# x times g fed to the first 27 projection units in quarters, with 1/rms applied to their products

## The chip, the cores and the metric

One core of a Trainium2 chip runs the whole kernel. The time is the device time of that core in microseconds (us); less is better. Before the change it is 2242.05 us, the median of 3 runs.

## What is computed

One inference step of a decoder layer with two token mixers, in float32. There are 288 tokens (256 of a prompt, 32 of 8 sampled sequences of 4) and D_MODEL is 2048. What matters here is how it begins:

```
h    = x * rsqrt(mean(x*x) + 1e-6) * g_mix          # RMSNorm, per token
proj = h @ w_in                                     # all projections of both mixers
pb       = proj[..., N_IN_A:]                       # 3360 columns: 3 LoRA inputs, r, k, v
pb_first = h_prev @ w_in[:, N_IN_A:]                # h_prev: state_shift, already normalised
pb_prev  = concat([pb_first, pb[:, :-1]])
xm       = pb + (pb_prev - pb) * mu_b               # token shift
```

Then come the RWKV-7 state, sparse attention with an indexer, two branch projections, a gated merge, an output projection, and a SwiGLU block. h of each sequence's last token is an output too (shift).

## The kernel before

Everything is transposed: partitions are channels, tokens are columns. The weights come as units of 128 output channels, 1 MB each (128 partitions by 16 k-tiles of 128 columns), through a ring of four slots in SBUF. SyncE issues their loads, each when the unit four before it has been read. The first 27 units (3 for the LoRA inputs, 8 each for r, k and v) are those whose product is mixed with that of the previous token; they are the part that the change touches.

A unit of these is a float32 product in three passes. ScalarE copies the weight to a rounded upper half (`first_high`, L953), VectorE subtracts to get the lower half, in place in the ring (`first_low`, L1382), and TensorE does, for each k-tile, upper by upper, lower h by upper weight, and upper h by lower weight (`first_unit`, L454 to L456), 48 matmuls into one of two PSUM banks. The columns are NX = 296: the 288 tokens and 8 columns of state_shift.

Then ScalarE copies the product, shifted by one token, from PSUM to SBUF (`previous`, L974 to L976), and VectorE does the mixing with two operations that read the bank (`mix`, L1413 and L1415), the second of which frees it. Only then may TensorE fill that bank with the unit after the next. The upper halves of the weights have two buffers, so `first_high(u + 2)` waits until unit u has been read. All order is by counting semaphores and by the order of the code on each engine.

What comes ahead of unit 0: SyncE loads x (L309), the constants, the parameters (g_mix among them), the 8 state columns, the page table and the LoRA weights, and then units 0 to 3. ScalarE squares x in four pieces (L948), TensorE sums the squares over channels with a matrix of ones (`total_squares`, L466, which waits for all the small loads, since the ones are among the constants), VectorE forms the mean (L1366), ScalarE the root (L961), VectorE the reciprocal (L1368), and then VectorE forms h with one operation for each k-tile (`normed`, L1371), ScalarE its upper half (L964) and VectorE the lower (`first_h_low`, L1386), in groups of four k-tiles.

```
for u, dst in enumerate((SW, SG[:, 0, :], SG[:, 1, :])):
    first_low(u + 2, u + 3)
    mix(u, u % 2, dst)
```

After unit 7's load SyncE fetches 16 pages of indexer keys (L346), and goes on with unit 8. After unit 26, TensorE does the LoRA products (L486), ScalarE their sigmoids (L1001), and a long chain on VectorE follows (from L1444).

## Time and profile before

| | |
|---|---|
| median of 3 runs | 2242.05 us (2241.3 to 2242.24) |
| profiled execution, its time | 2239.98 us |
| profiled execution, its span | 2237.8 us |
| mean granted TensorE clock | 0.955 |
| TensorE (PE) busy | 2086.7 us, 93% |
| VectorE (DVE) busy | 1007.9 us, 45% |
| ScalarE (ACT) busy | 738.5 us, 33% |
| GpSimd (POOL) busy | 36.8 us, 2% |

The span is the stretch from the first to the last recorded instruction; the execution's time is 2.2 us longer. The engines work side by side, so their busy times don't add up. Since matmuls are pipelined, a busy TensorE is not TensorE at its peak. PEld is the load of weights into the array, SPq the issuing of transfers by SyncE.

### The profile page before, as it was taken

How to read it: one execution, taken by the hardware profiler on the slowest of the kernel's cores; microseconds unless marked ns; L12 is line 12 of the kernel's file. 1: busy time of each engine (PE TensorE's matmuls, PEld its weight loads, DVE VectorE, ACT ScalarE, POOL GpSimd, SP SyncE). 2: the span in 40 equal slices, each digit the busy share in tenths (PEclk: the TensorE clock that was granted, in tenths of full speed). 3: DMA queues.
4: the chain of work that ended last, by engine and by line, in shares of the span. 5: the costliest groups of instructions: out<-in, count | busy, mean ns of one | idle time of the engine just before them, and what ended most of it. 6: DMA issues, size and time to landing. Idle time of an engine off the chain costs nothing.

```text
span 2237.8 us, 38450 instructions
## 1 busy us (share of the span) xinstructions
PE 2086.7 (93%) x15718; PEld 1862.7 (83%) x15718; DVE 1007.9 (45%) x1161; ACT 738.5 (33%) x953; POOL 36.8 (2%) x59
## 2 busy tenths in 40 slices
PE   5999967999998989988998997999999999999996
PEld 4999745658885855558998997999999999999995
DVE  4454966717665601024454344444444444333333
ACT  3333202352323200023443233444454444233332
POOL 0000002100000000000000000000000000000000
PEclk9999987899998998888999998999999999999998
DMA  5444353324531399973445452444444444554452
GB/s 190 158 167 152 111 187 98 84 87 142 176 125 66 105 379 362 369 287 113 169 165 196 145 198 91 160 164 166 169 169 165 160 164 167 172 167 160 163 168 81
DMA packets 96821, 375.69 MB, mean 168 GB/s; under 512 B 27954, under 2 KB 38834, under 8 KB 69234
## 3 DMA queue, kind: packets, MB, share of 16 engines
q1 hardware_dynamic: 70626, 335.36, 43.0%
q10 hardware_dynamic: 21152, 19.66, 2.7%
q0 software_dynamic: 4976, 19.71, 2.5%
q8 instruction: 49, 0.80, 0.1%
q14 instruction: 18, 0.15, 0.0%
HBM read 358.14 MB, written 16.53 MB: 167 GB/s over the span
## 4 chain that ended last, share of the span: by engine, by line
PE 85%; DVE 7%; DMA 3%; ACT 2%; issue 2%; SPq 2%; ACTq 0%; POOL 0%; DVEq 0%; POOLq 0%
PE ps L420 13%; PE ps L912 13%; PE ps L913 13%; PE ps L914 12%; PE ps L871 5%; PE ps L872 4%; PE ps L873 4%; PE ps L454 2%; PE ps L455 2%; PE ps L456 2%; PE ps L812 2%; PE ps L844 1%; DMA gram<-arena 1%; PE ps L856 1%; PE ps L576 1%
## 5 line engine op out<-in xcount | busy, mean ns | idle before, releaser
L1766 DVE TENSOR_TENSOR weights_lo<-ring,weights_hi 128x2048 fp32r<-128x2048 f32 (+1 forms) x152 | 305.5, 2010 | 466.2 <-ACT weights_hi L1314 466.2
L912 PE MATMUL ps<-h_hi,weights_hi 128*128 128x288 f32 x1408 | 415.4, 295 | 15.4 <-DVE h_lo L1775 15.4
L913 PE MATMUL ps<-h_lo,weights_hi 128*128 128x288 f32 x1408 | 416.9, 296 | 0.0
L914 PE MATMUL ps<-h_hi,weights_lo 128*128 128x288 f32 x1408 | 413.3, 294 | 0.0
L420 PE MATMUL ps<-hT,ring 128*128 128x288 f32 x1472 | 381.2, 412 | 1.2 <-ACT arena L1083 1.2
L1314 ACT ACTIVATE weights_hi<-ring 128x2048 fp32r<-128x2048 f32 (+1 forms) x152 | 257.0, 1691 | 342.5 <-PE ps L914 341.0
L420 PEld LDWEIGHTS ps<-hT,ring 128*128 128x128 f32 x1472 | 273.8, 191 | 79.8 <-issue 7.0
L912 PEld LDWEIGHTS ps<-h_hi,weights_hi 128*128 128x128 f32 x1408 | 265.0, 188 | 15.8 <-DVEq L1790 15.8
L914 PEld LDWEIGHTS ps<-h_hi,weights_lo 128*128 128x128 f32 x1408 | 265.8, 189 | 0.0
L913 PEld LDWEIGHTS ps<-h_lo,weights_hi 128*128 128x128 f32 x1408 | 265.2, 188 | 0.0
L912 PE MATMUL ps<-act_hi,weights_hi 128*128 128x288 f32 x704 | 209.1, 297 | 4.9 <-DVE act_lo L1800 4.9
L913 PE MATMUL ps<-act_lo,weights_hi 128*128 128x288 f32 x704 | 208.3, 296 | 0.0
L914 PE MATMUL ps<-act_hi,weights_lo 128*128 128x288 f32 x704 | 207.5, 295 | 0.0
L1683 DVE TENSOR_TENSOR weights_lo<-ring,mix_weights_hi 128x2048 fp32r<-128x2048 f32 x48 | 110.0, 2292 | 143.3 <-ACT mix_weights_hi L1245 143.3
L454 PE MATMUL ps<-first_h_hi,first_weights_hi 128*128 128x296 f32 x432 | 131.2, 304 | 14.3 <-DVE first_h_lo L1386 10.6
L1245 ACT ACTIVATE mix_weights_hi<-ring 128x2048 fp32r<-128x2048 f32 x48 | 91.8, 1913 | 141.3 <-PE ps L873 141.3
L912 PEld LDWEIGHTS ps<-act_hi,weights_hi 128*128 128x128 f32 x704 | 132.5, 188 | 5.1 <-issue 5.1
L914 PEld LDWEIGHTS ps<-act_hi,weights_lo 128*128 128x128 f32 x704 | 133.2, 189 | 0.0
L913 PEld LDWEIGHTS ps<-act_lo,weights_hi 128*128 128x128 f32 x704 | 132.8, 189 | 0.0
L455 PE MATMUL ps<-first_h_lo,first_weights_hi 128*128 128x296 f32 x432 | 131.1, 303 | 0.0
L456 PE MATMUL ps<-first_h_hi,weights_lo 128*128 128x296 f32 x432 | 130.5, 302 | 0.0
L1382 DVE TENSOR_TENSOR weights_lo<-ring,first_weights_hi 128x2048 fp32r<-128x2048 f32 x27 | 61.9, 2292 | 106.8 <-ACT first_weights_hi L953 106.8
(333 smaller groups left out, 3041.0 us busy)
## 6 DMA issues: line engine op xcount, KB each, us to landing
ring<-in_wst SPq DMA_DIRECT2D x201, 1024.0 KB, 4.8
ring<-in_wdn SPq DMA_DIRECT2D x64, 704.0 KB, 4.0
arena<-in_kT SPq DMA_DIRECT2D x64, 512.0 KB, 5.5
arena<-in_v SPq DMA_DIRECT2D x64, 512.0 KB, 6.0
ring<-in_wst ACTq DMA_DIRECT2D x8, 1024.0 KB, 7.9
arena<-chunk_ar_bk ACTq DMA_DIRECT2D x24, 256.0 KB, 3.5
arena<-in_ki SPq DMA_DIRECT2D x64, 64.0 KB, 1.8
chunk_ar_bk<-arena POOLq DMA_DIRECT2D x2, 2048.0 KB, 14.3
```

Of the source, the lines that this page charges most:

```text
L420: ins = mm(out, ring[:, slot, k, :], rhs(k), start=(k == 0), stop=(k == KT - 1))
L454: mm(out, W_HI1[:, (u0 + s) % 2, w], H_HI1[:, k, :], start=(k == 0), stop=False)
L455: mm(out, W_HI1[:, (u0 + s) % 2, w], H_LO1[:, k, :], start=False, stop=False)
L456: ins = mm(out, W_LO[:, slot, w], H_HI1[:, k, :], start=False, stop=(k == KT - 1))
L871: mm(out, MW_HI[:, (u - U_MIX) % 2, w], hi, start=start, stop=False)
L912: mm(out, W_HI[:, (u - U_FF) % 2, w], hi, start=start, stop=False)
L913: mm(out, W_HI[:, (u - U_FF) % 2, w], lo, start=False, stop=False)
L914: return mm(out, W_LO[:, u % 4, w], hi, start=False, stop=stop)
L1245: fn(MW_HI[:, (u - U_MIX) % 2], ring[:, u % 4].rearrange("p k c -> p (k c)"), ACT.Copy).then_inc(sem("mix_w_high"), 1)
L1314: fn(W_HI[:, (u - U_FF) % 2, 0:n], ring[:, u % 4].rearrange("p k c -> p (k c)")[:, 0:n], ACT.Copy).then_inc(sem("w_high"), 1)
L1683: tt(W_LO[:, u % 4], raw, MW_HI[:, (u - U_MIX) % 2].bitcast(F32), ALU.subtract).then_inc(sem("mix_w_split"), 1)
L1766: tt(W_LO[:, u % 4, 0:m], raw, W_HI[:, at, 0:m].bitcast(F32), ALU.subtract).then_inc(sem("w_split"), 1)
```

## The change

x is loaded in four quarters of four k-tiles, each with its 8 state columns, behind the parameters and with unit 0's weight between the second and the third; the constants, the page table and the LoRA weights come behind unit 3. The units are fed not with h but with x times g: ScalarE forms the upper half of x times g (a copy with g as its scale), VectorE the lower half in one operation from x, g and the upper half. 1/rms is a factor of each token, so it may be applied to the product: `scaled` (L1442) multiplies a unit's bank by it on the way from PSUM to one of two SBUF buffers (NRM) and frees the bank, and `previous` and `mix` read NRM. For the state columns the factor is 1. The squares are made by GpSimd; TensorE sums the first half of them ahead of unit 0 and the second between units 0 and 1, with a matrix of ones that VectorE sets. h itself, which later stages need, is formed by VectorE two k-tiles a unit in units 3 to 10, and the shift output is taken at unit 11. VectorE's loops over the units are written out.

```
-        RSTD = area(33216, NT)
-        XT = area(16384, KT, NT)
+        XT = area(16640, KT, NX)
...
-        LAST = area(16384 + 4608, KT, 1 + NB)
+        LAST, ONE1 = area(23680, KT, 1 + NB), area(23840, P)
+        NRM, RSX = area(28672, 2, NX), area(29264, NX)
...
-            sp.dma_start(XT, xT[:, :, 0:NT]).then_inc(sem("x_in"), 16)
-            sp.dma_start(cst[:, :], cst_d).then_inc(sem("const_in"), 16)
-            sp.dma_start(prm[:, :], prm_d).then_inc(sem("const_in"), 16)
-            sp.dma_start(hT[:, :, NT:NX], xT[:, :, NT:NX]).then_inc(sem("const_in"), 16)
-            sp.dma_start(ptab[:, :], pt_d).then_inc(sem("const_in"), 16)
-            sp.dma_start(LORA, lora_d[0]).then_inc(sem("lora_in"), 16)
-
...
-            for u in range(4):
+            def x_group(g):
+
+                sp.dma_start(XT[:, 4 * g:4 * g + 4, :], xT[:, 4 * g:4 * g + 4, :]).then_inc(sem(f"x_in{g}"), 16)
+
+            sp.dma_start(prm[:, :], prm_d).then_inc(sem("prm_in"), 16)
+            x_group(0)
+            x_group(1)
+            unit(0, 0)
+            x_group(2)
+            x_group(3)
+            for u in range(1, 4):
                 unit(u, u)
+            sp.dma_start(cst[:, :], cst_d).then_inc(sem("const_in"), 16)
+            sp.dma_start(ptab[:, :], pt_d).then_inc(sem("const_in"), 16)
+            sp.dma_start(LORA, lora_d[0]).then_inc(sem("lora_in"), 16)
             units(4, 8, unit)
-            sp.wait_ge(sem("const_in"), 64)
-            sp.wait_ge(sem("h_done"), 1)
+            sp.wait_ge(sem("const_in"), 32)
...
-                        pe.wait_ge(sem("first_h_split"), k // 4 + 1)
+                        pe.wait_ge(sem("first_h_split"), 5 * (k // 4 + 1))
...
+            def squares_group(g):
+
+                pe.wait_ge(sem("squares"), g + 1)
+                for k in range(4 * g, 4 * g + 4):
+                    ins = mm(ps[7][:, 0:NT], ONE1, SQ[:, k, :], start=(k == 0), stop=(k == KT - 1))
+                if g == 3:
+                    ins.then_inc(sem("squares_summed"), 1)
+
             pe.sem_inc(sem("bank_free"), 2)
             pe.sem_inc(sem("chunk_done"), 1)
-            pe.wait_ge(sem("const_in"), 64)
-            total_squares(0, SQ)
-            for u in range(3):
-                first_unit(u, 0, 0)
+            pe.wait_ge(sem("dve_chain"), 1)
+            squares_group(0)
+            squares_group(1)
+            first_unit(0, 0, 0)
+            squares_group(2)
+            squares_group(3)
+            first_unit(1, 0, 0)
+            first_unit(2, 0, 0)
...
+            pe.wait_ge(sem("const_in"), 32)
+            pe.wait_ge(sem("h_done"), 1)
...
-            act.wait_ge(sem("x_in"), 16)
-            squares(XT, SQ)
+            def first_h_high(g):
+
+                act.wait_ge(sem(f"x_in{g}"), 16)
+                for k in range(4 * g, 4 * g + 4):
+                    fn(H_HI1[:, k, 0:NT], XT[:, k, 0:NT], ACT.Copy, scale=p_("g_mix", k)).then_inc(
+                        sem("first_h_high"), 1)
+                fn(H_HI1[:, 4 * g:4 * g + 4, NT:NX], XT[:, 4 * g:4 * g + 4, NT:NX], ACT.Copy).then_inc(
+                    sem("first_h_high"), 1)
+
+            act.wait_ge(sem("prm_in"), 16)
+            first_h_high(0)
+            first_h_high(1)
             first_high(0)
+            first_h_high(2)
+            first_h_high(3)
             first_high(1)
+            act.wait_ge(sem("unit_read"), 1)
+            first_high(2)
             act.wait_ge(sem("mean_sq"), 1)
-            fn(RSTD, RSTD, ACT.Sqrt).then_inc(sem("root"), 1)
-            for g in range(4):
-                act.wait_ge(sem("h_group"), g + 1)
-                fn(H_HI1[:, 4 * g:4 * g + 4, :], hT[:, 4 * g:4 * g + 4, :], ACT.Copy).then_inc(
-                    sem("first_h_high"), 1)
+            fn(RSX[:, 0:NT], RSX[:, 0:NT], ACT.Sqrt).then_inc(sem("root"), 1)
...
             def previous(u, par):
-                act.wait_ge(sem("unit_read"), u + 1)
-                act.wait_ge(sem("bank_free"), u + 1)
-                bank, pv = ps[par], PV[:, par, :]
+                act.wait_ge(sem("bank_free"), u + 3)
+                bank, pv = NRM[:, par, :], PV[:, par, :]
...
             for u in range(3):
-                act.wait_ge(sem("unit_read"), u + 1)
-                first_high(u + 2)
+                if u:
+                    act.wait_ge(sem("unit_read"), u + 1)
+                    first_high(u + 2)
+                if u == 2:
+                    act.wait_ge(sem("mixed"), 1)
                 previous(u, u % 2)
-            act.wait_ge(sem("bank_free"), 2 + 3)
+            act.wait_ge(sem("mixed"), 3)
             fn(SW[0:64, :], SW[0:64, :], ACT.Tanh).then_inc(sem("act_stage"), 1)
             ch(fn(SG, SG, ACT.Sigmoid))
             with act.Fori(0, 5) as i:
                 for s in range(4):
                     act.wait_ge(sem("unit_read"), i * 4 + (U_RKV + s + 1))
                     first_high(U_RKV + s + 2, i, 4)
+                    act.wait_ge(sem("mixed"), i * 4 + (U_RKV + s - 1))
                     previous(i * 4 + (U_RKV + s), (U_RKV + s) % 2)
...
-                rstd = RSTD if n == 0 else SG[:, 0, :]
+                rstd = SG[:, 0, :]
...
             def normed(dst, src, g, k):
-                return stt(dst[:, k, 0:NT], src[:, k, :], p_(g, k), RSTD if g == "g_mix" else SG[:, 0, :],
+                return stt(dst[:, k, 0:NT], src[:, k, 0:NT], p_(g, k), RSX[:, 0:NT] if g == "g_mix" else SG[:, 0, :],
                            ALU.mult, ALU.mult)
 
+            ch(nc.vector.memset(ONE1, 1.0))
+            ch(nc.vector.memset(RSX, 1.0))
...
             def first_h_low(g):
-                dve.wait_ge(sem("first_h_high"), g + 1)
-                tt(H_LO1[:, 4 * g:4 * g + 4, :], hT[:, 4 * g:4 * g + 4, :],
-                   H_HI1[:, 4 * g:4 * g + 4, :].bitcast(F32), ALU.subtract).then_inc(sem("first_h_split"), 1)
-
+                dve.wait_ge(sem("first_h_high"), 5 * (g + 1))
+                for k in range(4 * g, 4 * g + 4):
+                    stt(H_LO1[:, k, 0:NT], XT[:, k, 0:NT], p_("g_mix", k), H_HI1[:, k, 0:NT].bitcast(F32), ALU.mult,
+                        ALU.subtract).then_inc(sem("first_h_split"), 1)
+                old = slice(4 * g, 4 * g + 4)
+                tt(H_LO1[:, old, NT:NX], XT[:, old, NT:NX], H_HI1[:, old, NT:NX].bitcast(F32),
+                   ALU.subtract).then_inc(sem("first_h_split"), 1)
+
+            first_h_low(0)
+            first_h_low(1)
             first_low(0, 1)
-            first_low(1, 2)
-            dve.wait_ge(sem("const_in"), 64)
-            inv_rms(0)
-            for k in range(KT):
-                ins = normed(hT, XT, "g_mix", k)
-                if k % 4 == 3:
-                    ins.then_inc(sem("h_group"), 1)
-                else:
-                    ch(ins)
-                if k in (7, 11):
-                    first_h_low(k // 4 - 1)
-            dve.wait_ge(sem("h_group"), 4)
             first_h_low(2)
             first_h_low(3)
-            ch(cp(LAST[:, :, 0:1], hT[:, :, SEQ - 1:SEQ]))
-            cp(LAST[:, :, 1:], hT[:, :, SEQ:NT].rearrange("p k (b t) -> p k b t", t=NS)[:, :, :, NS - 1]).then_inc(
-                sem("h_done"), 1)
-
-
-            def mix(u, par, dst, rows=P):
+            first_low(1, 2)
+            dve.wait_ge(sem("squares_summed"), 1)
+            ts(RSX[:, 0:NT], ps[7][:, 0:NT], 1.0 / DM, EPS, ALU.mult, ALU.add).then_inc(sem("mean_sq"), 1)
+            first_low(2, 3)
+            dve.wait_ge(sem("root"), 1)
+            ch(nc.vector.reciprocal(RSX[:, 0:NT], RSX[:, 0:NT]))
+
+            def scaled(u):
+                dve.wait_ge(sem("unit_read"), u + 1)
+                tt(NRM[:, u % 2, :], ps[u % 2][:, 0:NX], RSX, ALU.mult).then_inc(sem("bank_free"), 1)
+
+            def mix(u, dst):
                 dve.wait_ge(sem("previous"), u * 3 + 3)
-                dve.wait_ge(sem("bank_free"), u + 2)
-                bank = ps[par][:, 0:NT]
-                ch(tt(DIF, PV[:, par, :], bank, ALU.subtract))
-                mu = prm[:, bass.ds(u + PRM["mu"][0], 1)]
-                stt(dst, DIF[0:rows], mu[0:rows], bank[0:rows], ALU.mult, ALU.add).then_inc(sem("bank_free"), 1)
+                if u:
+                    dve.wait_ge(sem("mixed"), u)
+                now = NRM[:, u % 2, 0:NT]
+                ch(tt(DIF, PV[:, u % 2, :], now, ALU.subtract))
+                stt(dst, DIF, p_("mu", u), now, ALU.mult, ALU.add).then_inc(sem("mixed"), 1)
 
             def flat(a):
                 return a.rearrange("p a n -> p (a n)")
 
-            for u, dst in enumerate((SW, SG[:, 0, :], SG[:, 1, :])):
-                first_low(u + 2, u + 3)
-                mix(u, u % 2, dst)
-            with dve.Fori(0, 4) as i:
-                ch.enter(i, 4)
-                for s in range(4):
-                    first_low(U_RKV + s + 2, i * 4 + (U_RKV + s + 3))
-                    mix(i * 4 + (U_RKV + s), (U_RKV + s) % 2, flat(RK[:, bass.ds(i * 4 + s, 1), :]))
-            ch.leave(4)
-            for j in range(CT):
-                u = U_RKV + 2 * CT + j
-                if u + 2 < U_IDX:
+            for u in range(U_IDX):
+                scaled(u)
+                if 3 <= u + 2 < U_IDX:
                     first_low(u + 2, u + 3)
-                mix(u, u % 2, V[:, j, :])
-            dve.wait_ge(sem("bank_free"), 2 + 27)
+                if u < 3:
+                    dst = (SW, SG[:, 0, :], SG[:, 1, :])[u]
+                elif u < U_RKV + 2 * CT:
+                    dst = RK[:, u - U_RKV, :]
+                else:
+                    dst = V[:, u - U_RKV - 2 * CT, :]
+                mix(u, dst)
+                if 3 <= u < 3 + KT // 2:
+                    for k in range(2 * (u - 3), 2 * (u - 2)):
+                        ch(normed(hT, XT, "g_mix", k))
+                if u == 3 + KT // 2:
+                    ch(cp(LAST[:, :, 0:1], hT[:, :, SEQ - 1:SEQ]))
+                    cp(LAST[:, :, 1:], hT[:, :, SEQ:NT].rearrange("p k (b t) -> p k b t", t=NS)[:, :, :, NS - 1]).then_inc(
+                        sem("h_done"), 1)
+            dve.wait_ge(sem("mixed"), U_IDX)
...
         @block.gpsimd
         def _(pool):
+            for g in range(4):
+                pool.wait_ge(sem(f"x_in{g}"), 16)
+                part = XT[:, 4 * g:4 * g + 4, 0:NT]
+                nc.gpsimd.tensor_tensor(SQ[:, 4 * g:4 * g + 4, :], part, part, ALU.mult).then_inc(sem("squares"), 1)
```

Three places of the order. First ScalarE from its start: L948 are the squares, L953 and L972 the upper halves of weights, L964 and L979 the upper halves of h or of x times g (L981 for the state columns), L961 and L994 the root. Before:

```order
L948 ACT_TABLE_LOAD
L948 ACTIVATE arena<-arena 128x1152 [waits x_in]
L948 ACTIVATE arena<-arena 128x1152 x3
L953 ACTIVATE first_weights_hi<-ring 128x2048 [waits w_in0]
L953 ACTIVATE first_weights_hi<-ring 128x2048 [waits w_in1]
L961 ACT_TABLE_LOAD
L961 ACTIVATE arena<-arena 128x288 [waits mean_sq]
L964 ACTIVATE first_h_hi<-hT 128x1184 [waits h_group] x4
```

and with the change:

```order
L979 ACT_TABLE_LOAD [waits x_in0]
L979 ACTIVATE first_h_hi<-arena,prm 128x288 [waits prm_in]
L979 ACTIVATE first_h_hi<-arena,prm 128x288 x3
L981 ACTIVATE first_h_hi<-arena 128x4x8
L979 ACTIVATE first_h_hi<-arena,prm 128x288 [waits x_in1]
L979 ACTIVATE first_h_hi<-arena,prm 128x288 x3
L981 ACTIVATE first_h_hi<-arena 128x4x8
L972 ACTIVATE first_weights_hi<-ring 128x2048 [waits w_in0]
L979 ACTIVATE first_h_hi<-arena,prm 128x288 [waits x_in2]
L979 ACTIVATE first_h_hi<-arena,prm 128x288 x3
L981 ACTIVATE first_h_hi<-arena 128x4x8
```

The squares are gone from ScalarE, the four large copies have become twenty, the first two quarters stand ahead of unit 0's weight, and the table load has the wait for the first quarter.

Second, VectorE from its first weight or lower half on. Before (L1382 lower half of a weight, L1366 and L1368 mean and reciprocal, L1371 h, L1386 its lower half):

```order
L1382 TENSOR_TENSOR weights_lo<-ring,first_weights_hi 128x2048 [waits first_high,dve_chain]
L1382 TENSOR_TENSOR weights_lo<-ring,first_weights_hi 128x2048 [waits first_high]
L1366 TENSOR_SCALAR arena<-ps 128x288 [waits squares_summed,const_in]
L1368 RECIPROCAL arena<-arena 128x288 [waits root]
L1371 SCALAR_TENSOR_TENSOR hT<-arena,prm 128x288 [waits dve_chain] x4
L1371 SCALAR_TENSOR_TENSOR hT<-arena,prm 128x288
L1371 SCALAR_TENSOR_TENSOR hT<-arena,prm 128x288 [waits dve_chain] x3
L1386 TENSOR_TENSOR first_h_lo<-hT,first_h_hi 128x1184 [waits first_h_high]
L1371 SCALAR_TENSOR_TENSOR hT<-arena,prm 128x288
```

and with the change (L1422 and L1425 lower half of x times g, L1417 of a weight):

```order
L1422 SCALAR_TENSOR_TENSOR first_h_lo<-arena,prm,first_h_hi 128x288 [waits first_h_high,dve_chain]
L1422 SCALAR_TENSOR_TENSOR first_h_lo<-arena,prm,first_h_hi 128x288 x3
L1425 TENSOR_TENSOR first_h_lo<-arena,first_h_hi 128x4x8
L1422 SCALAR_TENSOR_TENSOR first_h_lo<-arena,prm,first_h_hi 128x288 [waits first_h_high]
L1422 SCALAR_TENSOR_TENSOR first_h_lo<-arena,prm,first_h_hi 128x288 x3
L1425 TENSOR_TENSOR first_h_lo<-arena,first_h_hi 128x4x8
L1417 TENSOR_TENSOR weights_lo<-ring,first_weights_hi 128x2048 [waits first_high]
L1422 SCALAR_TENSOR_TENSOR first_h_lo<-arena,prm,first_h_hi 128x288 [waits first_h_high]
L1422 SCALAR_TENSOR_TENSOR first_h_lo<-arena,prm,first_h_hi 128x288 x3
```

Mean, reciprocal and h no longer stand ahead of the lower halves; two quarters stand ahead of unit 0's weight.

Third, VectorE in the units. Before, units 1 and 2:

```order
L1382 TENSOR_TENSOR weights_lo<-ring,first_weights_hi 128x2048 [waits first_high]
L1413 TENSOR_TENSOR arena<-arena,ps 128x288 [waits bank_free,previous]
L1415 SCALAR_TENSOR_TENSOR small<-arena,prm,ps 128x288 [waits dve_chain]
L1382 TENSOR_TENSOR weights_lo<-ring,first_weights_hi 128x2048 [waits first_high]
L1413 TENSOR_TENSOR arena<-arena,ps 128x288 [waits bank_free,previous]
L1415 SCALAR_TENSOR_TENSOR small<-arena,prm,ps 128x288 [waits dve_chain]
```

and with the change, unit 3 and the first two rows of unit 4 (L1442 is `scaled`, L1449 and L1450 the mixing, L1404 h):

```order
L1442 TENSOR_TENSOR arena<-ps,arena 128x296 [waits unit_read]
L1417 TENSOR_TENSOR weights_lo<-ring,first_weights_hi 128x2048 [waits first_high]
L1449 TENSOR_TENSOR arena<-arena 128x288 [waits mixed,previous]
L1450 SCALAR_TENSOR_TENSOR arena<-arena,prm 128x288 [waits dve_chain]
L1404 SCALAR_TENSOR_TENSOR hT<-arena,prm 128x288
L1404 SCALAR_TENSOR_TENSOR hT<-arena,prm 128x288 [waits dve_chain]
L1442 TENSOR_TENSOR arena<-ps,arena 128x296 [waits unit_read,dve_chain]
L1417 TENSOR_TENSOR weights_lo<-ring,first_weights_hi 128x2048 [waits first_high]
```

The operation that frees the bank stands ahead of the weight's lower half now, and behind it before.

## Rows read from the trace of the kernel before

**Rows 1.** The page: the chain that ended last, its shares by engine.
```profile
PE 85%; DVE 7%; DMA 3%; ACT 2%; issue 2%; SPq 2%; ACTq 0%; POOL 0%; DVEq 0%; POOLq 0%
```

**Rows 2.** Timeline, 0 to 62: start, duration, engine, line, what [idle before, releaser].
```profile
0.72 1.28 ACT L948 ACT_TABLE_LOAD   x1 [0.72 <-PEq L1935]
0.73 0.69 SPq L309 DMA_DIRECT2D arena<-in_xT  x1
...
5.91 8.21 SPq L313 DMA_DIRECT2D ptab<-in_pt  x1
10.54 4.32 ACT L948 ACTIVATE arena<-arena 128x1152 f32<-128x1152 f32 x4 [8.54 <-DMA arena<-in_xT]
...
15.17 10.53 PE L466 MATMUL ps<-arena,cst 128*128 128x288 f32 x32 [15.17 <-DMA ptab<-in_pt]
20.12 1.91 ACT L953 ACTIVATE first_weights_hi<-ring 128x2048 fp32r<-128x2048 f32 x1 [5.26 <-DMA ring<-in_wst]
22.14 2.29 DVE L1382 TENSOR_TENSOR weights_lo<-ring,first_weights_hi 128x2048 fp32r<-128x2048 f32 x1 [20.70 <-ACT first_weights_hi L953]
22.73 1.91 ACT L953 ACTIVATE first_weights_hi<-ring 128x2048 fp32r<-128x2048 f32 x1 [0.69 <-DMA ring<-in_wst]
...
27.84 1.95 DVE L1368 RECIPROCAL arena<-arena 128x288 f32<-128x288 f32 x1 [0.51 <-ACT arena L961]
29.83 4.27 DVE L1371 SCALAR_TENSOR_TENSOR hT<-arena,prm 128x288 f32<-128x288 f32 x8
...
34.02 1.38 DVE L1386 TENSOR_TENSOR first_h_lo<-hT,first_h_hi 128x1184 fp32r<-128x1184 f32 x1
...
35.55 0.58 PE L454 MATMUL ps<-first_h_hi,first_weights_hi 128*128 128x296 f32 x1 [9.85 <-DVE first_h_lo L1386]
```

**Rows 3.** Windows: stretch, length, busy (x) by engine, granted clock, DMA share, GB/s.
```profile
15.00:20.00 5.00, 4.83 (x10) 3.53 (x11) 0.00 (x0) 0.00 (x0) 0.00 (x0) 1.00 0.95 365
20.00:25.70 5.70, 5.70 (x23) 4.05 (x21) 3.32 (x2) 4.87 (x3) 0.00 (x0) 1.00 1.02 428
...
30.50:31.00 0.50, 0.00 (x0) 0.00 (x0) 0.47 (x2) 0.00 (x0) 0.00 (x0) 0.50 0.00 0
35.50:40.50 5.00, 4.95 (x19) 4.62 (x20) 4.79 (x9) 1.19 (x1) 0.00 (x0) 0.50 0.00 0
...
45.95:52.50 6.55, 6.55 (x50) 6.55 (x49) 3.17 (x3) 2.33 (x4) 0.00 (x0) 1.00 0.47 161
```

**Rows 4.** The chain in order of time at unit 8, then two windows there.
```profile
65.59 0.33 SPq L317
...
85.19 4.98 DMA ring<-in_wst
...
94.35 0.46 DVE arena L1413
94.98 0.53 DVE arena L1415
95.64 0.58 PE ps L454
...
92.30:95.00 2.70, 0.01 (x1) 0.00 (x0) 2.52 (x3) 2.57 (x7) 0.00 (x0) 1.00 0.97 388
...
96.00:98.50 2.50, 2.50 (x12) 2.50 (x12) 2.32 (x3) 0.00 (x0) 0.00 (x0) 0.50 0.48 187
```

**Rows 5.** The page's DMA issues: KB each, median us from issue to landing.
```profile
ring<-in_wst SPq DMA_DIRECT2D x201, 1024.0 KB, 4.8
...
arena<-in_ki SPq DMA_DIRECT2D x64, 64.0 KB, 1.8
```

**Rows 6.** Timeline of ScalarE and VectorE behind unit 26.
```profile
221.76 0.38 ACT L974 ACTIVATE arena<-ps 128x255 f32<-128x255 f32 x1 [6.01 <-PE ps L456]
...
222.40 7.18 ACT L1001 ACTIVATE arena<-ps,prm 128x288 f32<-128x288 f32 x16
...
236.48 14.55 DVE L1444 RECIPROCAL arena<-arena 128x2304 f32<-128x2304 f32 x1 [2.87 <-ACT arena L1005]
```

More of the change, by code:

```diff
@@ L994, in _ @@
                     first_high(u + 2)
+                act.wait_ge(sem("mixed"), u - 1)
                 previous(u, u % 2)
```

## The prediction

> **What bounds the kernel now.** The chain of waits over the whole span comes first: TensorE holds 85% of it [rows 1]. So an edit is worth what it moves the moment at which TensorE's work goes on, and nothing else. The change touches only the first 27 units (the first tenth of the span), and there I read the timeline from the start [rows 2]. The load of x is issued at 0.73 and lands at 10.54; TensorE starts at 15.17, released by the page table's load, whose issue alone held SyncE's queue from 5.91 to 14.12; the 16 products with ones take 10.53; then comes a serial stretch on VectorE: two weight splits, the reciprocal (1.95), 16 products for h at 4.27 for eight, and four lower halves of h at 1.38. TensorE's first product of unit 0 starts at 35.55.
>
> The windows show the clock [rows 3]. From 15.00 to 20.00 TensorE gets through 10 matmuls of the ones product, and in the next 5.70 through 23: half the pace, though the granted clock is printed as 1.00. TensorE fell idle at 25.7 (15.17 + 10.53); by 30.50 the granted clock is 0.50 (1.2 instead of 2.4 GHz), and it still is over the first 5.0 after TensorE's restart. After that a unit of 48 matmuls takes 6.55. Unit 0 ends at 45.95, where the row of a unit begins, so unit 2 ends at 59.05. I use that moment as the yardstick.
>
> There is one more hole, at unit 8 [rows 4]. SyncE issues unit 7's load at 65.59, then 16 pages of indexer keys, and only then, at 85.19, unit 8's. That weight's lower half is there at 94.35, and behind it VectorE does the two mixing operations of unit 6 (until 95.5) which free the PSUM bank that unit 8 wants. TensorE does next to nothing from 92.30 on, at a granted clock of 1.00 up to 95.00, restarts at 95.64, and has 0.50 from 96.00 to 98.50.
>
> **The change, part by part.** *The loads.* A 1 MB unit lands 4.8 after its issue, a 64 KB page 1.8 [rows 5]; two units in one train land 2.6 apart (20.12 and 22.73 [rows 2]). A quarter of x is 606 KB, so some 1.5 each in a train. With the parameters' load issued at 0.73 and the first quarter at about 1.2: 1.2 + 1.8 + 1.5, and 1.0 for the parameters and for the slow start of an empty queue (estimate) gives 5.5. Then 7.0 for the second quarter, 9.6 for unit 0, 11.1, 12.6, and 15.2 for unit 1. The constants, the page table and the LoRA weights come behind unit 3 and are needed much later; the page table's 8.21 of queue time would now hold back only unit 4, which can't be issued before unit 0 is read. That costs nothing.
>
> *ScalarE.* Its table load, 1.28 at 0.72 so far, now stands behind the wait for the first quarter: 5.5 to 6.8. A scaled copy of 288 elements costs 0.45 (the sigmoids, 16 in 7.18 [rows 6]) and the four samples' copies little, so 1.9 a quarter: quarters 0 and 1 by 10.6, W-high of unit 0 (1.91) by 12.5, quarters 2 and 3 by 16.3.
>
> *VectorE.* Four operations of 0.53 and a small one are 2.3 a quarter, a weight's lower half 2.29. Alone it would do quarter 0 from 8.8 to 11.1, quarter 1 by 13.4, unit 0's weight by 15.7, quarters 2 and 3 by 20.3, unit 1's weight by 22.6.
>
> *GpSimd.* Its price is in no row: in this stage it runs no elementwise operation. The lower bound is VectorE's two-operand operation, 1.38 for 1184 elements, so 1.35 for 1152; the upper one the dearest elementwise row, the reciprocal, 1.95 for 288, so 7.8. I take 2.5, near the lower end, since the operation is of the cheap row's kind. The Trainium skill (GPSIMD Engine Reference, section 3.1) gives 4.5 us for 2048 such elements, which as an estimate is 2.5 here too; no run here shows it yet.
>
> *Both together.* Squares and lower halves each read two operands from SBUF at the same time, which no stretch of this trace shows. Bounds: they don't disturb each other, or each instruction has the memory to itself and they take turns. Taking turns, the squares run 5.5 to 8.0 and 8.0 to 10.5; VectorE, ready at 8.8, gets one operation in before the third (11.0 to 13.5), one before the fourth (14.0 to 16.5), and then has quarter 0 done at 17.8, quarter 1 at 20.1, the weight at 22.4, quarter 2 at 24.7, quarter 3 at 27.0. Undisturbed it is 15.7 for the weight. No row decides between them. Since both engines would read two operands each, of the same quarters, in the same microseconds, I take turns as the likelier case, and keep both ends. The Trainium skill (SBUF — State Buffer, section on SBUF's two separate sides) says VectorE and GpSimd share one pair of ports as an exclusive lock for a whole instruction when VectorE has two SBUF inputs; no run here shows it yet.
>
> *TensorE.* The ones products for quarters 2 and 3 now stand between units 0 and 1: 8 of 16, 4.0 at full pace (23 halves of such a product in 5.70 [rows 3]). Taking turns: TensorE has been idle since about 14, so 22.5 starts at half clock. The first eight k-tiles take 5.5 (20 of 24 matmuls in 5.0 at half pace), the next two groups of 12 some 1.65 each: unit 0 ends at 31.3, the squares at 35.3, unit 1 at 41.9, unit 2 at 48.4. Against 59.05 that is 10.6 earlier. Undisturbed: start 15.8, unit 0 ends at 22.4 (quarter 3 is there at 20.3), unit 2 at 39.5, 19.5 earlier. The mean, the root, the reciprocal and the first scaling take 0.46 + 0.45 + 1.95 + 0.46 after the squares, with a 2.29 weight between them: about 6 of the 6.55 of unit 1, so unit 2's bank is free in time.
>
> *Every unit.* VectorE gains a 0.46 operation from PSUM and, in units 3 to 10, two of 0.53. It has 2.29 + 0.46 + 0.52 per 6.55 now, so 4.8 with all: covered. If it were not, the lower half of unit u+2, ready 4.4 after unit u ends, would have 2.1 to spare.
>
> *Unit 8.* The bank is freed by the scaling, ahead of the weight's split, so TensorE restarts at 94.45 in the old times: 1.2 less. The clock fell only after 95.00; if TensorE's restart comes before that and it no longer falls, the stretch at half pace, 2.5 by the window and about 3 with its edges, gives 1.5 more. I count 2.7. Ends: 1.2 and 2.7.
>
> *The end of the stage.* ScalarE's last three copies (221.76 [rows 6]) now wait for a scaling of 0.46 and its release, and the 16 sigmoids and table loads behind them lead straight to VectorE's reciprocal at 236.48. That costs 0.6; it is the one place where the change adds to the path. From there all goes on as before, earlier.
>
> **Sum.** 10.6 + 2.7 - 0.6 = 12.7. The profiled execution took 2239.98 (its span 2237.8); it would be 2227.3. The median of the three runs is 2242.05, 2.07 above, and the forecast is for a median: 2229.3.
>
> **The rivals.**
> *A, undisturbed.* GpSimd and VectorE don't hinder each other: 19.5 + 2.7 - 0.6 = 21.6, so 2220.4. For it: no engine in the trace is seen to slow another. Against it: here two engines do two-operand reads of the same tile for the first time. Between this and the forecast lies a mere slowing, some 2225.
> *B, GpSimd is dear.* All four squares stand before VectorE's lower halves when turns are taken, and each microsecond more of a square delays TensorE's first unit by four. At 5.7 a square (2.5 + 12.7 / 4) the gain is gone, at 6.8 the kernel is slower by 0.2%, at the upper bound of 7.8 unit 0's weight is split at 42.6 and the time is about 2250. For it: nothing shows GpSimd's pace. Against it: it would have to be over four times the VectorE row.
> *C, it doesn't do what it says.* The first quarter lands no earlier than the whole did, because the small parameters' load ahead of it and the queue's start take most of the 10: then only the unblocked queue and the shorter serial stretch count. Starting 5 later, at 2234.
>
> **How the numbers follow.** Taking turns as computed 0.46, A 0.30, between them 0.12, C or a price of a square up to 5 (gains of 4.5 to 9) 0.05, no change 0.03, B 0.04. Within 0.2% (4.5) is what a measurement of this kernel can't tell from no change. So faster 0.93, same 0.03, slower 0.04. The range goes from A with 2 more (an earlier landing, a warmer clock), 2218, to turns with a square of 3.5, 2233.
>
> **What would show it.** The first quarter's wait on ScalarE ends at 5 to 6. GpSimd's four squares, with their mean. VectorE's lower halves: 0.53 each if A holds, stretched or held back to about 17 if turns are taken. TensorE's first product of unit 0 at 22.5 (A: 15.8) and unit 2's end at 48.4 (A: 39.5). The hole before unit 8 is 2.1 long with the clock at 1.00 behind it. Behind unit 26, ScalarE's copies start some 0.5 later after TensorE's last product than before. Wrong would be: a hole in TensorE between units 3 and 26 that was not there, or a later stage that doesn't start earlier by the same amount.

## The result and the profile after

| | before | after |
|---|---|---|
| median | 2241.68 us (4 runs, 2240.98 to 2242.24) | 2222.45 us (4 runs, 2221.03 to 2224.28) |
| ratio | | 0.9921, 95% interval 0.9905 to 0.9938 |
| profiled execution, span | 2239.98, 2237.8 | 2222.53, 2220.6 |

The kernel became 19.2 us faster by the medians and 17.45 by the two profiled executions. A second comparison of the same two kernels, made later, gave 2220.61 (6 runs) against 2240.07 (11 runs), ratio 0.9918 (0.9901 to 0.9934). The forecast was 2229.3, range 2218 to 2233: its direction was right, and its time 6.9 too high.

The page's chain by engine answers to [rows 1]: TensorE holds the end as before, and SyncE has 1% where it had 2%.

```profile
PE 86%; DVE 7%; DMA 3%; ACT 2%; issue 1%; SPq 1%; POOL 0%; DVEq 0%; POOLq 0%; ACTq 0%
```

The timeline of after from 0 to 40 (start, duration, engine, line, what, in brackets the idle time before and the releaser), against [rows 2]:

```profile
1.18 0.90 SPq L331 DMA_DIRECT2D arena<-in_xT  x2
5.88 0.33 SPq L342 DMA_DIRECT2D ptab<-in_pt  x1
...
5.63 1.28 ACT L979 ACT_TABLE_LOAD   x1 [5.63 <-DMA arena<-in_xT]
6.93 1.81 ACT L979 ACTIVATE first_h_hi<-arena,prm 128x288 fp32r<-128x288 f32 x4
...
8.97 1.15 DVE L1422 SCALAR_TENSOR_TENSOR first_h_lo<-arena,prm,first_h_hi 128x288 fp32r<-128x288 f32 x1 [6.83 <-ACT first_h_hi L981]
8.97 2.44 DVE L1422 SCALAR_TENSOR_TENSOR first_h_lo<-arena,prm,first_h_hi 128x288 fp32r<-128x288 f32 x4 [6.83 <-ACT first_h_hi L981]
10.90 0.51 DVE L1422 SCALAR_TENSOR_TENSOR first_h_lo<-arena,prm,first_h_hi 128x288 fp32r<-128x288 f32 x1
11.43 2.36 DVE L1422 SCALAR_TENSOR_TENSOR first_h_lo<-arena,prm,first_h_hi 128x288 fp32r<-128x288 f32 x1
11.43 5.50 DVE L1422 SCALAR_TENSOR_TENSOR first_h_lo<-arena,prm,first_h_hi 128x288 fp32r<-128x288 f32 x4
16.95 2.28 DVE L1417 TENSOR_TENSOR weights_lo<-ring,first_weights_hi 128x2048 fp32r<-128x2048 f32 x1
19.16 1.79 DVE L1422 SCALAR_TENSOR_TENSOR first_h_lo<-arena,prm,first_h_hi 128x288 fp32r<-128x288 f32 x4
...
5.64 4.17 POOL L1877 TENSOR_TENSOR arena<-arena 128x1152 f32<-128x1152 f32 x2 [5.20 <-DMA arena<-in_xT]
10.97 4.79 POOL L1877 TENSOR_TENSOR arena<-arena 128x1152 f32<-128x1152 f32 x2 [1.17 <-DMA arena<-in_xT]
...
19.29 0.62 PE L459 MATMUL ps<-first_h_hi,first_weights_hi 128*128 128x296 f32 x1 [4.34 <-DVE weights_lo L1417]
28.06 4.04 PE L478 MATMUL ps<-arena 128*128 128x288 f32 x16
```

The first quarter of x lands at 5.6. Later, with GpSimd done, four lower halves of x g take 1.79 (a step of 0.43 each; a single one has a duration of 0.51). The four from 8.97 take 2.44 and the four from 11.43 take 5.50. The single rows show where: the one that starts at 8.97 ends at 10.12, which is 0.31 after GpSimd's second square is over (5.64 + 4.17 = 9.81); the one that starts at 11.43 lasts 2.36 and ends 0.31 after the third square (10.97 + 2.51 = 13.48). Between 9.81 and 10.97 GpSimd waits for the third quarter, and there VectorE gets through quarter 0: its fourth operation starts at 10.90. TensorE starts unit 0 at 19.29, not at 35.55.

The windows of after (stretch, length, busy and count by engine, granted clock, DMA share, GB/s), against [rows 3] and the clock in [rows 4]:

```profile
20.00:24.00 4.00, 4.00 (x18) 4.00 (x18) 4.00 (x10) 0.00 (x0) 0.00 (x0) 0.50 0.85 358
24.00:28.00 4.00, 4.00 (x31) 4.00 (x30) 1.07 (x1) 0.00 (x0) 0.00 (x0) 0.99 0.00 0
...
78.00:80.00 2.00, 0.00 (x0) 0.00 (x0) 1.97 (x1) 1.96 (x5) 0.00 (x0) 1.00 1.00 422
80.00:82.00 2.00, 1.62 (x12) 1.62 (x13) 1.93 (x5) 0.47 (x1) 0.00 (x0) 1.00 0.99 389
```

Unit 0 still starts at half clock (0.50, which is 1.2 GHz), until about 24. The hole at unit 8 is still there (2.4 long), but the granted clock stays 1.00 in it and behind it. The chain of after at that hole, which answers to [rows 4], and at the end of the changed stage (L503 and L486 are the LoRA products, L1034 and L1001 their sigmoids):

```profile
70.95 5.11 DMA ring<-in_wst
76.09 1.93 ACT first_weights_hi L972
78.03 2.30 DVE weights_lo L1417
...
80.38 0.40 PE ps L459
...
205.04 4.13 PE ps L503 x18
209.17 3.80 ACT arena L1034 x9
...
219.88 14.56 DVE arena L1483
```

and the chain of before at the stage's end:

```profile
221.68 4.13 PE ps L486 x18
225.81 3.76 ACT arena L1001 x9
```

The two mixing operations that stood between the lower half and TensorE are gone from the chain. The rows of ScalarE and VectorE behind unit 26, against [rows 6]:

```profile
205.66 0.41 ACT L1002 ACTIVATE arena<-arena 128x255 f32<-128x255 f32 x1 [5.91 <-DVE arena L1442]
206.19 6.78 ACT L1034 ACTIVATE arena<-ps,prm 128x288 f32<-128x288 f32 x16
219.88 14.55 DVE L1483 RECIPROCAL arena<-arena 128x2304 f32<-128x2304 f32 x1 [2.48 <-ACT arena L1038]
```

**Where the 17.45 came from.** VectorE's long reciprocal, the landmark at the end of the changed stage, starts at 219.88 instead of 236.48: 16.60 earlier. Unit 2 ends at 45.25 (there ScalarE's copy of the next weight starts) instead of 59.05, which is 13.80 of it. From TensorE's products behind unit 26 to the reciprocal it is 14.84 (from 205.04), and it was 14.80 (from 221.68): nothing gained or lost. The remaining 2.84 is the hole at unit 8. Behind the landmark the two executions take 2000.7 and 2001.3 to the span's end, and what lies outside the span is 0.25 shorter.

### The profile page after: what moved, and what is told of

It reads as the page before. It is cut to its first block, busy times and chain, and to the rows that moved or that the text cites. A ratio compares the mean times of both kernels' runs of the same rounds, so it can differ in the third digit from the quotient of the medians.

```text
span 2220.6 us, 38439 instructions
## 1 busy us (share of the span) xinstructions
PE 2084.1 (94%) x15718; PEld 1860.0 (84%) x15718; DVE 1026.8 (46%) x1206; ACT 739.0 (33%) x965; POOL 45.8 (2%) x63
## 4 chain that ended last, share of the span: by engine, by line
PE 86%; DVE 7%; DMA 3%; ACT 2%; issue 1%; SPq 1%; POOL 0%; DVEq 0%; POOLq 0%; ACTq 0%
PE ps L425 13%; PE ps L931 13%; PE ps L932 13%; PE ps L933 13%; PE ps L890 5%; PE ps L891 5%; PE ps L892 5%; PE ps L459 2%; PE ps L460 2%; PE ps L461 2%; PE ps L831 2%; PE ps L863 1%; DMA gram<-arena 1%; PE ps L875 1%; PE ps L567 1%
## 5 line engine op out<-in xcount | busy, mean ns | idle before, releaser
L931 PEld LDWEIGHTS ps<-h_hi,weights_hi 128*128 128x128 f32 x1408 | 265.1, 188 | 15.8 <-DVEq L1829 15.8
L459 PEld LDWEIGHTS ps<-first_h_hi,first_weights_hi 128*128 128x128 f32 x432 | 82.4, 191 | 7.5 <-DVE weights_lo L1417 7.5
```

What stands on the lines that cost most here:

```text
L459: mm(out, W_HI1[:, (u0 + s) % 2, w], H_HI1[:, k, :], start=(k == 0), stop=False)
L931: mm(out, W_HI[:, (u - U_FF) % 2, w], hi, start=start, stop=False)
```

## The experiments

T is the forecast's reading, that an operation of VectorE that reads two operands from SBUF and a square of GpSimd take turns; A is its rival, that they don't disturb each other. The expectations call the other side S: there is no exclusion, and VectorE's long operations have another cause, such as the quarters' landing in SBUF. Ten runs were made. "Start" is TensorE's first product of unit 0, "unit 2" its end, "hole" TensorE's idle time before unit 8 and what the granted clock does in it or shortly behind it, "landmark" the start of the reciprocal; the last column has the median and the number of executions.

| kernel | start | unit 2 | hole at unit 8 | landmark | landmark to span's end | time |
|---|---|---|---|---|---|---|
| before | 35.55 | 59.05 | 3.3, falls | 236.48 | 2001.3 | 2241.68 (4) |
| after | 19.29 | 45.25 | 2.4, clock stays | 219.88 | 2000.7 | 2222.45 (4) |
| after_again | 19.25 | 45.31 | 2.2, stays | 219.76 | 1999.4 | 2220.61 (6) |
| e1_quiet | 15.35 | 39.18 | 2.3, falls | 215.17 | 2002.1 | 2219.37 (4) |
| e2_fill | 15.60 | 39.45 | 2.8, falls | 217.11 | 1999.0 | 2217.89 (1) |
| e3_double | 22.52 | 48.98 | 2.2, stays | 223.35 | 2001.7 | 2226.78 (1) |
| e4_bank_late | 19.41 | 45.75 | 2.9, falls | 222.72 | 2000.8 | 2225.33 (1) |
| e5_pages | 19.63 | 45.62 | none | 217.53 | 2006.9 | 2221.73 (4) |
| e6_old_loads | 20.68 | 46.05 | 2.3, falls | 222.12 | 1998.6 | 2222.51 (1) |
| e7_table | 19.30 | 44.56 | 2.3, falls | 220.54 | 2002.4 | 2224.78 (1) |
| e9_whole | 24.11 | 49.48 | 2.1, falls | 225.31 | 1999.2 | 2226.40 (1) |
| e8_best | 15.45 | 39.30 | none | 211.22 | 1998.1 | 2210.91 (5) |

The part behind the landmark, which no edit touches, varies by several microseconds. So effects of 1 to 3 us are read from the landmarks, each from one profiled execution, and not from the times.

**e1_quiet: two of the four squares on ScalarE.** The first hunk is GpSimd's loop, the second ScalarE's stream, behind its copy of unit 1's weight. TensorE's wait for the last two squares goes over to `squares_b` with it.

```diff
-            for g in range(4):
+            for g in range(2):
...
             first_high(1)
+            for g in range(2, 4):
+                fn(SQ[:, 4 * g:4 * g + 4, :], XT[:, 4 * g:4 * g + 4, 0:NT], ACT.Square).then_inc(sem("squares_b"), 1)
```

> Theory T (GpSimd's square and VectorE's two-operand operation exclude each other): with GpSimd doing only the squares of quarters 0 and 1 and ScalarE those of 2 and 3, after unit 1's upper half, only VectorE's first lower half is still held (1.15 us, as in the changed kernel); the second quarter's four take 1.8 us in place of 5.50. TensorE's first product of unit 0 starts at 15.4 in place of 19.29, and since it last worked at about 14.9 its clock does not fall, which saves 2.4 more of unit 0. Unit 2 ends at 39.1 in place of 45.25: 6 less, near 2216.4. Rival S (VectorE's two operations of 2.36 us were held by something else that comes with the quarters' landing, such as the loads' writes to SBUF): they stay long, the start stays at 19.3, the time at 2222.

VectorE and TensorE in its timeline:

```profile
8.73 2.44 DVE L1425 SCALAR_TENSOR_TENSOR first_h_lo<-arena,prm,first_h_hi 128x288 fp32r<-128x288 f32 x4 [6.60 <-ACT first_h_hi L982]
11.20 1.79 DVE L1425 SCALAR_TENSOR_TENSOR first_h_lo<-arena,prm,first_h_hi 128x288 fp32r<-128x288 f32 x4
...
15.35 0.40 PE L459 MATMUL ps<-first_h_hi,first_weights_hi 128*128 128x296 f32 x1 [2.15 <-DVE weights_lo L1420]
```

With no square beside them, the four operations that took 5.50 take 1.79, which is 3.71 less. The start is 3.94 earlier, of which 0.24 is x's earlier landing: that leaves 3.70, the same number. The quarters' loads are the same as in after, so S fails with A: T holds, and its price in the changed kernel is 3.7 for these four. There is a second gain. TensorE now idles 2.15 before unit 0 instead of 4.34, its granted clock stays at 1.00, and from the start to unit 2's end it takes 23.83 instead of 25.96. Unit 2 ends 6.07 earlier, as expected (39.18, expected 39.1), but the landmark only 4.71, because at the hole the clock now falls. The time is 2219.37 against 2239.34 (7 runs), ratio 0.991 (0.9887 to 0.9933); 2216.4 was expected, and by the time alone this kernel can't be told from the changed one. e8_best below settles that. The windows of e1_quiet there:

```profile
72.00:74.00 2.00, 0.00 (x0) 0.00 (x0) 2.00 (x1) 1.98 (x4) 0.00 (x0) 1.00 1.10 426
74.00:75.50 1.50, 1.34 (x9) 1.34 (x10) 1.43 (x5) 0.23 (x1) 0.00 (x0) 0.97 0.84 279
75.50:78.50 3.00, 3.00 (x14) 3.00 (x13) 2.97 (x3) 0.64 (x3) 0.00 (x0) 0.50 0.48 197
```

**e2_fill: as e1_quiet, with four GpSimd fills in the place of the two squares.**

```diff
+            pool.wait_ge(sem("x_in2"), 16)
+            for n in range(4):
+                nc.gpsimd.memset(area(29600, 1800), 0.0).then_inc(sem("fill"), 1)
+                pool.wait_ge(sem("fill"), n + 1)
```

(ScalarE's root waits for the fills too. They end at 17.66, long before the mean is there, at 26.8.)

> e1_quiet, with four fills of 1800 elements on GpSimd from the landing of quarter 2 on; a fill writes and reads nothing. The Trainium skill (SBUF - State Buffer, on SBUF's two separate sides) limits the lock against a VectorE operation with two SBUF inputs to a GpSimd operation that reads SBUF. By that, VectorE's lower halves keep 0.51 us under the fills and the start stays where e1_quiet has it (15.4). If any GpSimd work excludes VectorE, each fill holds one operation for its length (some 1.5 us) and the start of unit 0 comes 3 to 6 later than in e1_quiet.

```profile
11.45 1.79 DVE L1426 SCALAR_TENSOR_TENSOR first_h_lo<-arena,prm,first_h_hi 128x288 fp32r<-128x288 f32 x4
...
11.07 6.59 POOL L1884 MEMSET arena<- 128x1800 f32 x4 [1.25 <-DMA arena<-in_xT]
```

GpSimd is busy for the whole stretch, and VectorE's four operations still take 1.79. So it isn't any work of GpSimd that holds VectorE up: squares, which read SBUF, do, and fills, which only write it, don't. Whether a GpSimd operation with one SBUF operand would do it was not tried. The Trainium skill (SBUF — State Buffer, section "SBUF: two separate sides") says that VectorE with two SBUF inputs is locked out only by a GpSimd operation that reads SBUF, for that whole instruction. The traces agree: 1.79 for four operations beside the fills, 2.36 for a single one beside a square. (The landmark is later than e1_quiet's by 1.94, because the clock fell before TensorE had started unit 8, and stayed at 0.50 from about 74 to 81.)

**e3_double: each of the last two squares done twice.** Nothing is left out; the added squares go to scratch.

```diff
+                if g > 1:
+                    nc.gpsimd.tensor_tensor(area(29600 + 4 * NT * (g - 2), 4, NT), part, part, ALU.mult)
```

> The changed kernel with each square of quarters 2 and 3 done twice (the first copy goes nowhere), two GpSimd instructions of 2.1 us more. Theory T: two more VectorE operations are held for 2.1 to 2.4 us each, four of them long in all; unit 0 starts 4.2 to 4.4 later, at 23.6, and unit 2 ends at 49.6. Rival S: no VectorE operation is longer than now, the start stays at 19.3; TensorE may wait only for the last squares.

```profile
10.96 9.20 DVE L1422 SCALAR_TENSOR_TENSOR first_h_lo<-arena,prm,first_h_hi 128x288 fp32r<-128x288 f32 x4
...
10.58 2.43 POOL L1878 TENSOR_TENSOR arena<-arena 128x1152 f32<-128x1152 f32 x1 [1.25 <-DMA arena<-in_xT]
12.97 2.32 POOL L1879 TENSOR_TENSOR arena<-arena 128x1152 f32<-128x1152 f32 x1
15.25 2.32 POOL L1878 TENSOR_TENSOR arena<-arena 128x1152 f32<-128x1152 f32 x1
```

The squares start 2.28 to 2.39 apart, and all four operations of VectorE are now held, one for each square: 9.20, which is 3.70 more for two squares. The start is 3.23 later though x landed 0.47 earlier, together 3.70. The expectation, 4.2 to 4.4, took each hold at a square's full length; a held operation costs that less its own step, 2.28 - 0.43 = 1.85. Two engines that alternate instruction by instruction, as T has it.

How long VectorE's instruction is doesn't matter. In after_again, e4_bank_late and e5_pages the third square happened to get in ahead of the small operation for the state columns (32 elements, 0.18 in after), and that one was held instead:

```profile
11.56 2.09 DVE L1426 TENSOR_TENSOR first_h_lo<-arena,first_h_hi 128x32 fp32r<-128x32 f32 x1
```

This row is from e5_pages. A mere sharing of bandwidth, the "between them" of the forecast, would have stretched so small an operation by little.

**e5_pages: units 8 and 9 loaded before the second batch's pages of indexer keys.**

```diff
             ki_pages(0)
+            units(8, 10, unit)
             ki_pages(1)
-            units(8, U_VKQ + 8, unit)
+            units(10, U_VKQ + 8, unit)
```

> The changed kernel with the index pages in two halves, eight after unit 7 and eight after unit 9. If the hole before unit 8 is SyncE's queue being held by 16 pages (17.6 us of it), unit 8's weight now lands some 5 before it is wanted and the hole of 2.4 us is gone: 2.4 less, near 2220.0. If it was the ring's slot or the transfers' own time, a hole of 2 or more stays, at unit 8 or at unit 10.

The hole is gone, and from unit 2's end to the landmark it takes 171.91 instead of 174.63: 2.7 less. The time doesn't show it: 2221.73, ratio 0.9921 (0.9901 to 0.994), where 2220.0 was expected. In the profiled execution the part behind the landmark is 2006.9, the longest of all. There the granted clock from 400 to 500 behind the landmark is 0.86, and 674 products of TensorE start; in all the other profiles it is 0.93, with 700 to 704. Inconclusive by the time, clear by the landmark.

**e4_bank_late: TensorE waits for the mixing again, as before the change.**

```diff
                 pe.wait_ge(sem("bank_free"), u + 1)
+                if u0 + s >= 2:
+                    pe.wait_ge(sem("mixed"), u - 1)
```

> The changed kernel, but TensorE may fill a bank again only when the unit two before it is mixed, as before the change (the scaling no longer frees the bank early). If the early release is what shortened the hole before unit 8, the hole grows from 2.4 to 3.4 us (0.46 + 0.52 behind the split of unit 8's weight), the first units stay within 0.3 us, and the clock behind the hole may or may not fall (0 or 1.5 more): VectorE's long reciprocal starts 1.0 to 2.5 later than the changed kernel's 219.88. If not, the hole stays at 2.4.

The chain of e4_bank_late at unit 8:

```profile
80.68 0.47 DVE arena L1451
81.17 0.53 DVE arena L1452
81.74 0.61 PE ps L461
82.35 0.25 PE ps L462
```

The two mixing operations are back in the chain, TensorE restarts at 81.74 instead of 80.38, at half clock, and the landmark is 2.84 later. Of this, 0.50 was lost before unit 2's end; from there to the landmark it is 2.34 (176.97 against 174.63). So 2.34 of the hole's 2.84 in the result come back. The hole is 2.9 long where 3.4 was expected, the first units lose 0.5 where at most 0.3 was expected, and the landmark is later than the expected 1.0 to 2.5.

**e6_old_loads: the transfers in the old order.** x in quarters, but the parameters behind the constants and units 0 to 3 last.

```diff
-            sp.dma_start(prm[:, :], prm_d).then_inc(sem("prm_in"), 16)
-            x_group(0)
-            x_group(1)
-            unit(0, 0)
...
+            for g in range(4):
+                x_group(g)
             sp.dma_start(cst[:, :], cst_d).then_inc(sem("const_in"), 16)
+            sp.dma_start(prm[:, :], prm_d).then_inc(sem("prm_in"), 16)
...
+            for u in range(4):
+                unit(u, u)
```

> The changed kernel with the transfers in the order of before (x, in its quarters, then constants, parameters, page table, LoRA weights, and only then units 0 to 3). ScalarE's first copy then waits for the parameters, behind 1.5 MB of constants, at about 13.4, unit 0 lands at 17, GpSimd's squares are all done before VectorE starts (no VectorE operation is held), and unit 0 starts at 21.4: 2.1 later than the changed kernel's 19.29; unit 2 ends at 47.3. If the reordering is what matters most, it is 5 or more later.

```profile
12.67 1.81 ACT L976 ACTIVATE first_h_hi<-arena,prm 128x288 fp32r<-128x288 f32 x4 [6.67 <-DMA prm<-in_prm]
...
14.70 1.80 DVE L1419 SCALAR_TENSOR_TENSOR first_h_lo<-arena,prm,first_h_hi 128x288 fp32r<-128x288 f32 x4 [12.57 <-ACT first_h_hi L978]
...
4.71 8.29 POOL L1874 TENSOR_TENSOR arena<-arena 128x1152 f32<-128x1152 f32 x4 [4.28 <-DMA arena<-in_xT]
```

ScalarE's first copy waits for the parameters and starts 5.7 later than in after (12.67, 6.93), yet unit 0 starts only 1.39 later (20.68; 21.4 was expected). By 13.0 the squares are over, and VectorE is held up nowhere: the difference, 4.3, is what the held operations cost in after (2.44 and 5.50 instead of 1.79 twice). The order of the transfers and the turns on SBUF hide each other.

This run settles one more thing. The page table's load took 8.21 to issue in before, 0.33 in after, and 0.34 here, where it stands behind the constants and the parameters as in before (at 3.85). So the 8.21 were not its own price, and not one of the order. They went with the way x and its state columns are loaded: before, with 288 of its 296 columns, and the other 8 by a transfer of their own. In the first 20 us DMA moved 4737 packets in before, 2146 of them under 512 bytes, and 1404 here, 147 of them under 512 bytes. Which of the two loads held the queue, no run shows.

**e7_table: ScalarE's table loaded early by a copy of one element.**

```diff
+            act.wait_ge(sem("dve_chain"), 1)
+            fn(area(29600, 1), ONE1[:, 0:1], ACT.Copy)
             act.wait_ge(sem("prm_in"), 16)
```

> The changed kernel with ScalarE's table load (1.28 us) brought ahead of the wait for x by a one-element copy. Theory T (turns): VectorE's first lower half is ready 1.3 earlier, at 7.6, but meets the squares of quarters 0 and 1, and later those of 2 and 3 as now: two operations are held for over 2 us all the same, the start of unit 0 stays within 0.5 of 19.29 (18.8 to 19.8). Rival S (no exclusion; ScalarE's table load on the path to the start counts in full): unit 0 starts at 18.0.

```profile
7.70 3.72 DVE L1424 SCALAR_TENSOR_TENSOR first_h_lo<-arena,prm,first_h_hi 128x288 fp32r<-128x288 f32 x4 [5.56 <-ACT first_h_hi L981]
...
11.44 5.50 DVE L1424 SCALAR_TENSOR_TENSOR first_h_lo<-arena,prm,first_h_hi 128x288 fp32r<-128x288 f32 x4
```

VectorE starts 1.27 earlier, is held by two squares instead of one (3.72 instead of 2.44), and is where it was at 11.4: start 19.30, where T expected 18.8 to 19.8 and S 18.0. The 1.28 of the table load stand in the chain and are worth nothing at the start. Unit 2 ends 0.69 earlier all the same, as the granted clock is at 0.50 only up to 22.5 (24.1 in after); at the hole it falls, and the landmark is 0.66 later than in after.

**e9_whole: everything waits for the whole of x, which is loaded ahead of unit 0.**

```diff
             act.wait_ge(sem("prm_in"), 16)
+            for g in range(4):
+                act.wait_ge(sem(f"x_in{g}"), 16)
```

(GpSimd the same; and SyncE's `unit(0, 0)` stands behind `x_group(3)`.)

> The changed kernel without the feeding by quarters: ScalarE and GpSimd wait for all four quarters, which are loaded ahead of unit 0 (landing at about 10.0). ScalarE's first copy at 11.3, three VectorE operations held by squares (each up to 2.3 us), unit 0 starts at 23.9, 4.6 later than now, and unit 2 ends at 49.9. If the squares in turns were not on the path, it would start at 21.5 or before.

Start 24.11, unit 2's end 49.48: the quarters are worth 4.2 of the 13.8 at the start. The other 9.6 come with the rest: no sum of squares that unit 0 waits for, no 1/rms and no page table ahead of it. No run takes these apart. Three operations of VectorE are held (four take 6.23 from 13.70).

**e8_best and after_again: e1_quiet and e5_pages together, beside the changed kernel on one chip.**

> ScalarE squares quarters 2 and 3 (as in e1_quiet) and the index pages are split (as in e5_pages). Unit 0 starts at 15.4, unit 2 ends at 39.2, no hole before unit 8: VectorE's long reciprocal starts at 211.3 (219.88 less 6.1 less 2.4), and since no hole is left there is no clock to lose in it. 8.5 less than the changed kernel on the same chip, and some 27 less than the kernel before.

> The changed kernel once more, beside the next one: about 19 less than before, and the same landmarks as in its first trace (unit 0 starts at 19.3, unit 2 ends at 45.3) within 0.5, since the loads' landing varies by that. The hole before unit 8 is 2.2 to 2.8 long; whether the clock falls there is open.

e8_best took 2210.91 (5 runs, 2209.9 to 2211.8) against 2240.07, ratio 0.987 (0.9853 to 0.9887): 29.2 faster than before and 9.7 faster than the changed kernel (2219.25 to 2225.57), so both gains show in the time as well. Its landmark, 211.22 (expected 211.3), is 8.54 earlier than after_again's: 6.01 up to unit 2's end, and 2.53 for the hole, which is gone. Its windows where the hole would be:

```profile
70.00:74.00 4.00, 4.00 (x31) 4.00 (x30) 2.12 (x5) 1.88 (x2) 0.00 (x0) 1.00 0.79 268
74.00:78.00 4.00, 4.00 (x32) 4.00 (x31) 3.87 (x5) 0.56 (x4) 0.00 (x0) 1.00 0.56 233
```

## Why the prediction was right, and where its sizes were off

The direction and the mechanism were right. That the time was in the range is in part luck: the range's lower end came from A, which didn't hold, and the time is 6.85 below the forecast, three quarters of the way to A's 2220.4. The terms give the 6.85 back: 3.2 at the start (13.80 gained, forecast 10.6), 0.14 at the hole, 0.56 at the stage's end (forecast a loss of 0.6, measured 0.04), 0.85 behind the landmark and outside the span, and 2.1 from the step "the median of the three runs is 2242.05, 2.07 above": the profiled execution of after stood at its own median (2222.53, 2222.45).

- *The loads.* First quarter at 5.6, forecast 5.5. Right. The "page table's 8.21 of queue time" was not that transfer's price (0.33 here, see e6_old_loads); the forecast needed nothing from it.
- *ScalarE.* Quarter 0 from 6.93, four copies in 1.81. Right. Its table load stands in the chain as forecast, and e7_table shows that it costs nothing there, which the forecast didn't see.
- *GpSimd.* "I take 2.5": two squares took 4.17 (2.10 each), the third, beside VectorE, 2.51. The choice near the lower bound was right. The Trainium skill's figure (GPSIMD Engine Reference, section 3.1), which gave 2.5 as an estimate, is above the undisturbed 2.10 of the trace.
- *Both together.* Turns, as forecast; e1_quiet, e2_fill, e3_double and e7_table each show it. Of the held operations' size the forecast was right: one per square. What failed is the step "gets one operation in before the third (11.0 to 13.5), one before the fourth": as the first two squares took 2.1 each, GpSimd was done at 9.81 and stood waiting until 10.97, and four of VectorE's operations went through. By the fourth square's end (15.76, forecast 16.5) VectorE had done five operations and begun the sixth, not two, and had 3.4 of work left ahead of unit 0 instead of 5.9. 0.7 and 2.5 make the 3.2 by which TensorE started earlier (19.29, forecast 22.5). The step of an operation was also mis-sized, 0.43 for "0.53".
- *TensorE.* It started at half clock as forecast, and the second set of ones products took 4.04 (forecast 4.0). From the start to unit 2's end it was 25.96, forecast 25.9.
- *Rival A.* It named 15.8 and 39.5; e1_quiet, where only VectorE's first operation is held, gave 15.35 and 39.18. It was the right price for a condition that didn't hold.
- *Rivals B and C.* A square at 2.1 to 2.5 and x at 5.6 rule them out. "Each microsecond more of a square delays TensorE's first unit by four" was too steep: e3_double's two added squares, 4.6 more of GpSimd, cost 3.7, and the 1.16 in which GpSimd waits for the third quarter would take up some growth of the first two (a longer square was not tried). B's "42.6" also leaves out VectorE's own turns between the squares; by the rival's rule it is 22.4 + 4 x 5.3 = 43.6.
- *Unit 8.* 2.7 forecast, 2.84 measured. Of the 1.2 for the freed bank e4_bank_late shows about 1 (its mixing ends at 81.70, the lower half of unit 8's weight at 80.76). The reason given for the 1.5, "if TensorE's restart comes before that and it no longer falls", doesn't hold in general: see below.
- *The end of the stage.* ScalarE's copies do start later behind TensorE's products (205.66 against 205.04; before 221.76 against 221.68), as forecast. But the copies are not on the path there. Both chains go from TensorE's products straight to the sigmoids, each of which waits for its own product, and the products set the pace: they run from 221.61 for 7.43 in before and from 204.97 for 7.46 in after, and the last sigmoid ends 0.54 after the last product in both (229.58, 212.97). The sigmoids start later and take 6.78 instead of 7.18 [rows 6], as they wait less for products. "It is the one place where the change adds to the path" is the step that failed here: it adds 0.04.
- No new hole appeared between units 3 and 26, and the rest of the kernel runs as before.

## What to carry to other kernels

Before work is spread over VectorE and GpSimd, look at what each reads: an operation of VectorE with two SBUF operands stands still for a whole GpSimd operation that reads SBUF (2.36 instead of 0.51 here), so count how many of the one fall beside the other. The length of VectorE's operation doesn't matter: one of 0.18 was held as one of 0.51 is. With half of the squares on ScalarE, unit 2 ended 6 us earlier: 3.7 from the turns, 2.1 from the clock, which then stayed up, and 0.2 from an earlier landing. Ask of every row in the chain whether something behind it would wait anyway, as the table load's 1.28 did. And where a short idle stretch of TensorE is left, close it instead of counting on its clock to stay up.
